# The attention stage of a two-layer hybrid decoder step: gate before the division, K V Q Z order, and evacuation moved to ScalarE

## The reference

```python
k, v, logf = shared_kv(x)              # from the residual stream x
p = h @ w_in + b_in                    # h = x * (1 + scale) + shift
q, z = p[..., :FA_WIDTH], p[..., FA_WIDTH:]
logits = q . k * 64 ** -0.5 + c_q - c_k      # causal; c = cumsum(logf)
o = softmax(logits) @ v
y = (o * silu(z)) @ w_out + b_out
x = layer_norm(alpha * x + (1 + gate) * y)
```

## Time and profile before

| quantity | value |
|---|---|
| median of three runs | 2117.64 us |
| the profiled execution | 2118.48 us |
| its span, first to last instruction | 2117.0 us |
| PE busy | 1869.0 us, 88% |
| DVE busy | 1041.0 us, 49% |
| ACT busy | 580.4 us, 27% |
| POOL busy | 365.2 us, 17% |

### The profile page before, as it was taken

The page is one execution under the profiler, slowest core; times in us unless marked ns, Lnnn a source line. Parts: engine busy times, 40 slices in busy tenths (PEclk is TensorE's granted clock), DMA queues, the critical chain, the costliest instruction groups (busy, mean ns, idle before and its releaser), DMA issues.

```text
span 2117.0 us, 27900 instructions
## 1 busy us (share of the span) xinstructions
PE 1869.0 (88%) x10256; PEld 1592.4 (75%) x10256; DVE 1041.0 (49%) x1583; ACT 580.4 (27%) x994; POOL 365.2 (17%) x401
## 2 busy tenths in 40 slices
PE   7999999999999899967987879788888888659888
PEld 2999989999999899965866767666666666437743
DVE  1432443323323431155356655665657575689753
ACT  0311121111111331144224333333343424252120
POOL 0000021101110000023022221313131313253120
PEclk9999999999999999988998988999899989679999
DMA  7111112222212122213210202020202020317591
GB/s 291 40 50 40 39 64 77 79 79 79 69 52 79 50 90 70 70 30 93 71 59 21 80 21 79 20 76 23 69 30 69 20 79 20 113 51 275 175 390 68
DMA packets 46589, 172.03 MB, mean 81 GB/s; under 512 B 6122, under 2 KB 6762, under 8 KB 45378
## 3 DMA queue, kind: packets, MB, share of 16 engines
q1 hardware_dynamic: 29202, 111.91, 15.5%
q0 software_dynamic: 17328, 59.33, 8.2%
HBM read 145.68 MB, written 17.15 MB: 77 GB/s over the span
## 4 chain that ended last, share of the span: by engine, by line
PE 73%; DVE 17%; issue 5%; ACT 3%; POOL 1%; DMA 0%; DVEq 0%; SPq 0%; ACTq 0%; POOLq 0%
PE bank L1470 17%; PE bank L1471 16%; PE bank L1472 16%; PE bank L1883 3%; PE bank L1569 3%; DVE rc L1261 3%; PE bank L1627 2%; DVE w_lo L871 2%; PE bank L1734 2%; PE bank L1685 2%; DVE rc L1260 2%; PE bank L1736 2%; PE bank L1735 2%; DVE bank L1226 1%; PE bank L1479 1%
## 5 line engine op out<-in xcount | busy, mean ns | idle before, releaser
L1470 PE MATMUL bank<-h_hi,w_lo 128*128 128x344 f32 x1152 | 373.5, 324 | 4.9 <-DVE h_lo L902 4.3
L1471 PE MATMUL bank<-h_lo,w_hi 128*128 128x344 f32 x1152 | 368.1, 320 | 0.0
L1472 PE MATMUL bank<-h_hi,w_hi 128*128 128x344 f32 x1152 | 367.8, 319 | 0.0
L1470 PE MATMUL bank<-x_hi,w_lo 128*128 128x512 f32 x528 | 232.2, 440 | 37.7 <-DVE y2T L1167 36.1
L486 POOL TENSOR_TENSOR p_lo<-parg,p_hi 128x512 fp32r<-128x512 f32 (+1 forms) x192 | 193.9, 1026 | 308.8 <-ACT p_hi L781 307.4
L1470 PEld LDWEIGHTS bank<-h_hi,w_lo 128*128 128x128 f32 x1152 | 217.1, 188 | 11.2 <-issue 8.6
L1471 PE MATMUL bank<-x_lo,w_hi 128*128 128x512 f32 x528 | 217.6, 412 | 0.0
L1471 PEld LDWEIGHTS bank<-h_lo,w_hi 128*128 128x128 f32 x1152 | 217.1, 188 | 0.0
L1472 PE MATMUL bank<-x_hi,w_hi 128*128 128x512 f32 x528 | 217.0, 411 | 0.0
L1472 PEld LDWEIGHTS bank<-h_hi,w_hi 128*128 128x128 f32 x1152 | 216.9, 188 | 0.0
L1470 PE MATMUL bank<-y_hi,w_lo 128*128 128x344 f32 (+1 forms) x512 | 175.7, 343 | 18.5 <-DVE y_lo L1193 11.3
(11 more groups left out here) (286 smaller groups left out, 3020.4 us busy)
## 6 DMA issues: line engine op xcount, KB each, us to landing
raw<-units SPq DMA_DIRECT2D x105, 512.0 KB, 3.3
ada_ring<-w_ada SPq DMA_DIRECT2D x32, 512.0 KB, 3.5
pages<-cache_k POOLq DMA_DIRECT2D x32, 512.0 KB, 5.2
pages<-cache_v POOLq DMA_DIRECT2D x32, 512.0 KB, 11.4
ada_first<-w_ada SPq DMA_DIRECT2D x8, 1024.0 KB, 12.0
ckb<-scr_c POOLq DMA_DIRECT2D x16, 512.0 KB, 5.1
KX<-KA SPq DMA_DIRECT2D x32, 256.0 KB, 4.3
xT<-x_t SPq DMA_DIRECT2D x1, 4128.0 KB, 28.1
```

The costliest lines, as they stand in the source:

```text
L1470: mm(out, lhs_lo, rhs_hi, start=first, stop=False)
L1471: mm(out, lhs_hi, rhs_lo, start=False, stop=False)
L1472: return mm(out, lhs_hi, rhs_hi, start=False, stop=last)
```

## The change

Six things change, all in the attention stage.

1. **Order K, V, Q, Z.** `KIND = (0, 2, 1, 3)` maps the place of a unit to its kind. The V transposes of pair 0 come after the second unit.
2. **Evacuation of K, V and Q by ACT** (`evac`), on bias and Identity; DVE keeps the sample columns and Z.
3. **Weights of Q and Z scaled by POOL**: `scale` multiplies `raw` by `one_p` into `w_sc`, in the memory of `w_lo`. ACT and DVE then split a unit with one instruction each.
4. **K and Q are split at the end of the phase before** (`kq_high(j + 1)`, `kq_low(j + 1)`).
5. **The gate is taken on the undivided sums**: `gate_o` is only two products (p @ v by silu(z)); ACT copies the sums of p out of banks 6 and 7 (`take_sums`). DVE takes reciprocals of these copies later, in two pieces of 128x256, and multiplies (`invert`, `divide_o`). For the second half this falls into the next phase, and the copy lies in `parg`, so `zth` no longer waits for it.
6. **The interleaving on PE** is written anew: 62 of the 64 steps now come before the phase's transposes instead of 61, the steps lie closer to the first half of the phase, and `scores` of chunk 11 comes two steps after `values` of chunk 9.

```diff
+        KIND = (0, 2, 1, 3)
+        def sums(half):
+            return rc[:, :] if half == 0 else parg[:, 0, :]
...
+            def scale(j, q, k0, k1):                                      # POOL
+                slot = (U_B + q) % 2
+                if k0 == 0:
+                    pool.wait_ge(S(f"raw_in{slot}"), 16 * (2 * j + (U_B + q) // 2 + 1))
+                    pool.wait_ge(S("mm"), 12 * j + 3 * q - 3)
+                ins = g.tensor_tensor(w_sc[:, slot, k0:k1, :], raw[:, slot, k0:k1, :], wide(one_p[:, k0:k1], P), ALU.mult)
...
             def phase(j):                                                 # POOL
+                store_k(j + 1)
+                scale(j + 1, 2, 0, KB)
                 for h in range(2):
                     pool.wait_ge(S("nl_ready"), 16 * j + 15 + h)
                     load_c(j + 1, h)
-                store_k(j + 1)
-                for c in range(12):
+                p_low(j, 0)
+                p_low(j, 1)
+                scale(j + 1, 3, 0, KB // 2)
+                p_low(j, 2)
+                scale(j + 1, 3, KB // 2, KB)
+                p_low(j, 3)
+                store_v(j + 1)
+                for c in range(4, 12):
                     p_low(j, c)
-                store_v(j + 1)
...
+            def take_sums(j, half):                                       # ACT
+                act.wait_ge(S("pv_done"), 24 * j + 8 + 16 * half)
+                A(sums(half)[0:HD, :], bank(6)[HD:P, :], ACT.Copy).then_inc(S("o_sums"), 1)
+                A(sums(half)[HD:P, :], bank(7)[0:HD, :], ACT.Copy).then_inc(S("o_sums"), 1)
...
-            def gate_o(j, half, more):                                    # DVE
+            def gate_o(j, half):
-                v.reciprocal(rc[0:HD, :], bank(6)[HD:P, :]).then_inc(S("o_nrm"), 1)
-                v.reciprocal(rc[HD:P, :], bank(7)[0:HD, :]).then_inc(S("o_nrm"), 1)
-                v.tensor_tensor(rc[:, :], rc[:, :], y2T[:, j, cs], ALU.mult).then_inc(S("o_nrm"), 1)
-                v.tensor_tensor(y2T[0:HD, j, cs], bank(6)[0:HD, :], rc[0:HD, :], ALU.mult)
-                v.tensor_tensor(y2T[HD:P, j, cs], bank(7)[HD:P, :], rc[HD:P, :], ALU.mult).then_inc(S("o_done"), 1)
+                v.tensor_tensor(y2T[0:HD, j, cs], bank(6)[0:HD, :], y2T[0:HD, j, cs], ALU.mult)
+                v.tensor_tensor(y2T[HD:P, j, cs], bank(7)[HD:P, :], y2T[HD:P, j, cs], ALU.mult).then_inc(S("o_step"), 1)
+            def invert(j, half, part):
+                ps_ = slice(part * HALF // 2, (part + 1) * HALF // 2)
+                v.reciprocal(sums(half)[:, ps_], sums(half)[:, ps_]).then_inc(S("o_step"), 1)
...
                 if c == 4:                                                # PE, values
-                    pe.wait_ge(S("o_done"), 2 * j + 1)
+                    pe.wait_ge(S("o_sums"), 4 * j + 2)
+                    pe.wait_ge(S("o_step"), 8 * j + 1)
...
                 values(j, 11)                                             # PE, end of phase
-                steps(60, 61)
                 if more:
                     transpose_vt(j + 1)
-                steps(61, 64)
+                steps(62, 64)
```

More of the change, by code:

```diff
@@ L580, in hi @@
                 A(w_hi[:, slot, :, :], raw[:, slot, :, :], ACT.Copy).then_inc(S("hi_ready"), 1)
-            def hi_scaled(u, slot, n, free, value, part=None):
-                if part != 1:
-                    act.wait_ge(S(f"raw_in{slot}"), 16 * n)
-                    wait(act, S(free), value)
-                for k in range(KB) if part is None else range(part * KB // 2, (part + 1) * KB // 2):
-                    last = A(w_hi[:, slot, k, :], raw[:, slot, k, :], ACT.Copy, scale=one_p[:, k:k + 1])
-                if part != 0:
-                    last.then_inc(S("hi_ready"), 1)
             act.wait_ge(S("c_in"), 16)
@@ L781, in probs @@
                     A(p_hi[:, r, off:HALF], parg[:, r, off:HALF], ACT.Copy).then_inc(S("p_hi"), 1)
-            for q in range(4):
-                split_hi((q + 1) // 4, (q + 1) % 4)
+            split_hi(0, 1)
+            evac(0, 0, 0)
+            evac(0, 0, 1)
+            split_hi(0, 2)
+            evac(0, 1, 0)
+            evac(0, 1, 1)
+            split_hi(0, 3)
+            evac(0, 2, 0)
+            evac(0, 2, 1)
+            split_hi(1, 0)
+            kq_high(0)
             z_tanh(0, 0)
@@ L813, in phase @@
                     z_tanh(j + 1, 0)
+                probs(j, 11)
+                if more:
+                    kq_high(j + 1)
+                take_sums(j, 1)
+                if more:
                     v_hi(j + 1)
@@ L1281, in _ @@
-            evac_kqv(0, 2, 1)
+            evac_s(0, 3)
             split_lo(1, 0)
-            evac_s(0, 3)
+            kq_low(0)
             z_evac(0, 0)
@@ L1288, in phase @@
             def phase(j, more):
-                kq_low(j)
+                if not isinstance(j, int) or j > 0:
+                    invert(j - 1, 1, 0)
+                    invert(j - 1, 1, 1)
+                    divide_o(j - 1, 1)
                 key_decay(j)
@@ L1348, in phase @@
                     score(5)
-                gate_o(j, 1, more)
+                exponents(j, 11)
+                if more:
+                    kq_low(j + 1)
+                gate_o(j, 1)
                 if more:
@@ L1813, in phase @@
+                scores(j, 10)
+                steps(57, 58)
+                values(j, 9)
+                steps(58, 59)
                 scores(j, 11)
-                steps(55, 57)
+                steps(59, 61)
                 values(j, 10)
-                steps(57, 60)
+                steps(61, 62)
                 values(j, 11)
-                steps(60, 61)
                 if more:
                     transpose_vt(j + 1)
-                steps(61, 64)
+                steps(62, 64)
```

288 lines of the change are left out of this document (163 added, 125 removed).

## The result

The changed kernel takes 1992.05 us (median of 4 runs, 1990.1 to 1993.37), the kernel before in the same comparison 2117.8 us (2113.8 to 2119.54). The ratio is 0.9408, with a 95% interval from 0.9392 to 0.9424: 5.9% faster. The forecast was 2007, the range 1968 to 2052. Direction and range were right.

What follows compares the result with a forecast made beforehand. PE sets the pace, and DVE where PE waits. The period falls from 109.1 to 94.2 us, saving 104 us over seven phases, plus 7.4 in phase 7: 2118.5 - 111 = 2007.5, or 2007 on the median's scale; range 1968 to 2052.

Steps and rivals of the forecast that it cites:

- What bounds, and the gate: PE sets the pace, DVE its waits; at chunk 4's `values` the gate wait and clock loss go, 11.4 us a phase.
- ScalarE's copies: At the first gate, two 64x512 copies of 0.65 us each; ACT is later than DVE, with 0.2 us to spare.
- ScalarE late at the gate: Rival: copies come one chunk's exponentials late and the clock falls; a phase gives back 5.8 us, 2048; chance 0.15.
- The phase's end: Next phase's first step waits 3.9 us for `z_evac` instead of 5.8; clock loss stays at 2.0 us.
- The wait of chunk 11: Near the phase's end, a new small wait as chunk 11's exponents stand behind `z_evac`'s first half; 0.8 us.
- The start of a phase: Splits leave DVE's head, reciprocals of 1.7 us and a product come; waits for `nminr` and `mb` go, 2.4 us.
- Evacuations and scaling "at nothing": Evacuations moved to ACT and scalings to POOL (4.1 us a phase) cost nothing, hidden by PE's work.
- the cover of 5.7 us: POOL's low parts of a chunk are wanted 5.7 us behind that chunk's scores, so they are hidden.
- The sum: Period falls from 109.1 to 94.2 us, 14.9 saved in each of phases 0 to 6; 111 us saved in all.
- No wait at the end: Rival: faster DVE hand-overs or a clock that holds gain up to 5.9 us more a phase, 1966; chance 0.12.
- GpSimd and DVE hold each other up: Rival: the scalings, 4.1 us a phase, fall wholly on DVE's chain or the low parts, 2036; chance 0.07.
- Phase 7: Last phase: two gates save 6.6 us, splits going for reciprocals coming save 0.8; 7.4 us in all.

Runs made afterwards that it cites:

- experiment 6: Changed kernel with ScalarE's rounding of the fourth unit's weights (1.06 us) moved ahead of the two copies of the first half's sums; 2003.26 us.
- experiment 4: Kernel of experiment 3 with the deferred reciprocals and product between peaks 4, 5 and 6, and eight PE steps instead of six before the first peak; 1965.49 us.
- experiment 10: Kernel of experiment 5 with one more PE step ahead of `values(0)`, the one that stood behind it; 1960.84 us.
- experiment 8: Changed kernel with the third and fourth units' weights scaled in eight pieces on ScalarE and eight on VectorE again, nothing scaled on GpSimd; 2033.9 us.
- experiment 7: Changed kernel with the six evacuations of K, V and Q on VectorE again (0.74 us each); 1986.62 us.
- experiment 5: Kernel of experiment 4 with K and Q of the last phase split at the end of the phase before, as in the changed kernel; 1963.31 us.
- experiment 12: Kernel of experiment 5 with V's first-half evacuation moved from ScalarE to VectorE, ahead of the third unit's low split, in each phase; 1962.8 us.
- experiment 3: Changed kernel with K and Q split at the head of the phase again, behind Z and not ahead of the last gate; 1989.85 us.
- experiment 11: Kernel of experiment 10 with all six evacuations on VectorE; 1967.26 us.

## Why the prediction was right, and where it was short

**What bounds, and the gate.** Right in the mechanism. The gate alone brings 100 us and undoing it alone costs 120. The forecast of 11.4 us for the first gate can't be separated from the end wait in these runs, since both experiments move both.

**ScalarE's copies.** 0.60 and 0.59 us for the estimated 0.65, and ScalarE was the later, as forecast. The margin of 0.2 us is nil by experiment 6: the count of PE's work up to there was right to that extent, and the rival "ScalarE late at the gate" was close. In phase 7 it came about once, with a wait of 2.4 us. At 1 us late it costs 1 us and no clock; the rival had 3.2 us of lateness, which no run made in phases 0 to 6, and 2.6 of clock behind it.

**The phase's end.** 4.24 us for the forecast 3.9, behind the very chain that was counted. The half clock behind it was put at 2.0. The window at 1514.86 gives 4.00 x (1 - 0.64) = 1.4, but that is the least of the six behind end waits: counted in the same way, as half of PE's busy time at half clock, they cost 1.4 to 3.0 us, 2.3 in the mean. The wait of chunk 11 was 0.27 us and not 0.8.

**The start of a phase.** The reciprocals of 128x256 take 1.75 us for 1.7, and `nminr` no longer ends a wait in phases 0 to 6. What experiment 4 adds: 24 us lay in their place ahead of the peaks together with the place of the splits, which the forecast held to be nearly free.

**Evacuations and scaling "at nothing".** This step failed in both directions. The scaling on GpSimd is worth 42 us in the changed order, since the scaled units now stand third and fourth, beside the low parts, where eight pieces would take 5 us and more; before, the second unit's pieces ran among the peaks. The right reading of the earlier trace rows was not that the new scaling could hurt but that the old split would have. The evacuations on ScalarE cost 5 us in the changed kernel, by where they left DVE's split (on top of experiment 10 the same move brought nothing). And a wait of 1.24 us for a low part came into every phase: the cover of 5.7 us that the forecast gave the low parts did not hold at `values(0)`, where DVE's split held up GpSimd.

**The sum.** Period: 93.55 for 94.2, 15.7 us saved for 14.9. PE's idle time in phases 1 to 6 fell from 18.3 to 6.3 us a phase, 12.0 less, where the forecast's terms make 12.3 (8.8 + 5.8 + 2.4 - 3.9 - 0.8). Single terms missed by more than that: the low part's 1.24 and the end wait's 0.3 came on top, while 0.5 at chunk 11 did not come and two waits of 0.38 and 0.28 us at `values(0)` of the phase of the earlier trace rows went. PE's busy time fell from 91.0 to 87.3, 3.7 less, and here the forecast had 2.6 of half clock. The forecast read one phase, and the phases differ. Two phases before in windows (us, PE busy, granted clock, DMA share, GB/s), and a stretch of the first:

```profile
1268.12:1378.47 110.35, 92.54 (x456) 0.90 0.15 48
1378.47:1486.66 108.19, 90.01 (x456) 0.91 0.16 48
1284.27:1291.09 6.82, 6.37 (x21) 0.50 0.00 0
```

The second is the phase of the earlier trace rows. The first has a third stretch at half clock, behind the wait for `nminr`, and so have phases 0, 4 and 6: with it half clock cost 7.3 to 7.4 us in a phase of the loop, without it 4.6 to 4.9. The wait for `nminr` thus had a clock loss behind it in every other phase, which the forecast put at nothing. That the period of the earlier trace rows was 0.9 us longer than the phase of the earlier trace rows was the sign of it.

*Phase 0* is the largest miss, 5.4 us. Before, PE's first step there waited 1.54 us and ran at half clock, 4.04 us of it; after, it waits 0.18 us and the clock is full:

```profile
1049.56:1053.60 4.04, 4.04 (x10) 3.17 (x11) 3.95 (x4) 3.97 (x8) 0.00 (x0) 0.50 0.01 2
```
```profile
1049.69 0.50 PE L1547 MATMUL bank<-x_hi,w_lo 128*128 128x512 f32 x1 [0.18 <-DVE y2T L1232]
```

The first row is of the kernel before, the second of the changed one. The whole phase, before and after:

```profile
1048.76:1159.66 110.90, 94.36 (x456) 0.88 0.15 48
```
```profile
1048.89:1139.53 90.64, 85.79 (x462) 1.00 0.18 58
```

PE's busy time fell by 8.6 us, 6.0 more than the 2.6 of the forecast, and its idle time by 11.7, 0.6 less than forecast: the miss is the clock, which was low in four stretches of this phase before and in none after. The forecast multiplied one loop phase by seven and never looked at the first. *Phase 7*: its head, to the rounding of `nminr`, took 15.4 us before and takes 10.5 now, where the forecast had 0.8 saved.

```profile
1702.44 3.37 PE L1821 MATMUL bank<-ident,kqvzS 128*8 128x128 f32 x16 [0.31 <-DVE y2T L1234]
...
1711.37 0.17 DVE L1297 CAST nminr<-nmin 128x8 fp32r<-128x8 f32 x1
```

PE's 3.37 us of transposes for the samples' q, and DVE's copy of them, used to stand between the peaks, where DVE idled 2.8 us for them. They now run beside the two reciprocals. The whole diff has this move (`tok` ahead of the peaks on DVE) and the forecast left it out. The rest of phase 7 saved 5.9 us for 6.6.

**The rivals.** None came about as a time. "No wait at the end" was refuted by the 4.24 us. "GpSimd and DVE hold each other up" is real as a mechanism: pieces of 0.35 us at the median take up to 1.39 in experiment 8, and GpSimd's second low part takes 2.24 us beside a DVE split and 1.28 without it. The Trainium skill, GPSIMD Engine Reference, "Key points", names DVE instructions with two inputs in SBUF among those that contend, and by the eviction from PSUM in experiment 7, beside which the low part took 1.28 us, the trace agrees. But the change was on the good side of it.

## What to carry to other kernels

Before an operation is called hidden, ask beside which engine's work it will run once the order around it has changed, and time it by the row where it ran in such company. Put what is deferred behind the work that the pacing engine waits for next, not ahead of it: here two reciprocals and a product placed between the peaks, with two of PE's steps moved, were worth 24 us more. And count the first and last turn of a loop apart, and read more than one turn of the middle: 8.5 of the 14 us that the forecast missed lay in the first and last, and most of the rest in half clock that the one turn it read didn't have.

## What the runs showed of the hardware that was not expected

**The clock fell behind waits of a microsecond and less that stood beside narrow matmuls.** A wait of 0.92 to 1.33 us just ahead of the 16 matmuls of 9 columns was followed by half clock in 13 of 14 cases (0.52 and 0.50 in the windows of experiment 8), at some 1.6 us more each, counted as above. A wait of 1.08 us amid matmuls of 512 columns left it at 1.00, seven times of seven. A wait of 0.48 to 0.50 us directly behind the narrow ones did either: the clock fell behind 9 of 18 in experiments 4, 5 and 12, and behind 12 of 18 in experiments 3, 10 and 11. Length alone doesn't decide: in experiment 3 a wait of 2.0 us for the sample columns' evacuation left the clock full in four phases of six. The Trainium skill, TensorE: Matmul & The Clock Gate, section "A second HAM failure mode: psum-queue depth-cycling", tells of a kernel in which PE's short idle times between groups of matmuls made the clock swing; by that the trace agrees. That the narrow matmuls are the cause is not shown: no run put other matmuls beside the same wait. Nor do the runs tell why one phase keeps its clock and the next loses it.

**Eight small instructions on DVE lost more beside GpSimd than one large.** Eight scaled splits of 128x128 (0.35 us each at the median, 2.8 together) became 5.73 us, while one split of 128x1024, 1.22 us at the median where it is not scaled (L953), took 1.49 and 1.58 in the changed kernel and 1.94 in experiment 7. The two differ in operation as well as in size, and which counts was not tested.
